# The first projection unit of a two-block transformer kernel stored as two blocks of 256 columns

## What is computed

```python
z = (x @ w_in).astype(F32)          # x: 256 x 1024, w_in: 1024 x 11016
zA, zB, zC, zD, zG = _split(z[..., :N_COLS_BASE], (RWKV_COLS, HGRN_COLS, MLSTM_COLS, LRU_COLS, GATE_COLS))
...
xr, gate = _split(zD, (BRANCH_WIDTH, BRANCH_WIDTH))   # 512 columns each
xc = _causal_conv(xr, conv_w, conv_b)
```

## Time and profile before

| | us |
|---|---|
| median of 3 runs | 1740.6 (1738.82 to 1742.21) |
| the profiled execution, its own time | 1739.38 |
| its span, first to last instruction | 1737.6 |
| PE busy in the span | 1700.8 (98%) |
| VectorE (DVE) busy | 570.5 (33%) |
| ScalarE (ACT) busy | 261.1 (15%) |
| bytes moved by DMA | 540.46 MB, 311 GB/s in the mean |

### The profile page before, as it was taken

How to read it: one execution, slowest core, us unless ns; L and a number is a source line. 1 busy time by engine, 2 the same in 40 slices (tenths; PEclk the granted TensorE clock), 3 DMA queues, 4 the chain that set the end, 5 groups by cost and what they waited for, 6 DMA issues and landing times.

```text
span 1737.6 us, 24288 instructions
## 1 busy us (share of the span) xinstructions
PE 1700.8 (98%) x10121; PEld 997.3 (57%) x10121; DVE 570.5 (33%) x1070; ACT 261.1 (15%) x446; POOL 28.9 (2%) x42
## 2 busy tenths in 40 slices
PE   8999999999999999999999999999999989999998
PEld 7787888888643433333333333433333338998885
DVE  2784377454341111111111111111121235536603
ACT  0323115002011111101010101101010121112200
POOL 1000000100000000000000000000000000000000
PEclk9999999999999999999999999999999999999999
DMA  8564332545799999999999999999999995532331
GB/s 320 191 257 183 146 122 100 166 164 191 270 404 424 421 424 427 427 427 428 428 427 428 426 428 427 428 428 427 426 428 427 428 418 205 194 146 102 141 143 46
DMA packets 65257, 540.46 MB, mean 311 GB/s; under 512 B 5514, under 2 KB 14276, under 8 KB 35744
## 3 DMA queue, kind: packets, MB, share of 16 engines
q1 hardware_dynamic: 58464, 527.31, 74.0%
q10 hardware_dynamic: 4560, 5.90, 1.2%
q0 software_dynamic: 2160, 6.17, 1.1%
HBM read 533.57 MB, written 5.78 MB: 310 GB/s over the span
## 4 chain that ended last, share of the span: by engine, by line
PE 91%; DMA 5%; DVE 2%; ACT 1%; issue 1%; SPq 0%; DVEq 0%; ACTq 0%
PE small L1440 24%; PE small L1482 12%; PE proj L816 10%; PE proj L1590 6%; PE proj L1002 5%; DMA arena<-in_expert_w_gu 4%; PE proj L1666 4%; PE proj L1415 3%; PE small L1388 3%; PE small L1427 2%; PE small L1447 2%; PE small L1081 2%; PE small L837 2%; PE proj L826 2%; PE proj L1529 2%; PE small L1547 2%
## 5 line engine op out<-in xcount | busy, mean ns | idle before, releaser
L1440 PE MATMUL small<-arena 128*64 128x512 f32 x2048 | 447.1, 593 | 6.8 <-DMA arena<-in_expert_w_gu 4.3
L1440 PEld LDWEIGHTS small<-arena 128*64 128x64 f32 x2048 | 151.1, 137 | 287.4 <-issue 274.5
L1482 PE MATMUL small<-arena 128*64 128x512 f32 x1024 | 226.8, 595 | 8.6 <-ACT arena L1924 7.9
L2593 DVE TENSOR_SCALAR arena<-small 128x512 f32<-128x512 f32 x32 | 22.1, 692 | 544.3 <-PE small L1447 544.3
L816 PE MATMUL proj<-arena 128*128 128x256 f32 x832 | 183.2, 380 | 0.9 <-DMA arena<-in_w_in_first 0.9
L816 PEld LDWEIGHTS proj<-arena 128*128 128x128 f32 x832 | 157.0, 190 | 23.1 <-DMA arena<-in_w_in_first 1.3
L1482 PEld LDWEIGHTS small<-arena 128*64 128x64 f32 x1024 | 74.5, 137 | 138.8 <-issue 138.8
L1590 PE MATMUL proj<-arena 128*128 128x128 f32 x896 | 100.5, 275 | 0.5 <-ACT arena L1982 0.5
L1590 PEld LDWEIGHTS proj<-arena 128*128 128x128 f32 x896 | 100.3, 192 | 1.1 <-ACT arena L1982 0.7
L1749 ACT ACTIVATE arena<-proj 128x512 f32<-128x512 f32 (+2 forms) x76 | 43.7, 593 | 361.1 <-PE proj L816 118.4
L1920 ACT ACTIVATE arena<-arena 128x512 f32<-128x512 f32 x32 | 20.1, 629 | 495.0 <-DVE arena L2593 495.0
(11 more groups left out here) (455 smaller groups left out, 1576.6 us busy)
## 6 DMA issues: line engine op xcount, KB each, us to landing
arena<-in_expert_w_gu SPq DMA_DIRECT2D x128, 2048.0 KB, 20.6
arena<-in_expert_w_down SPq DMA_DIRECT2D x31, 2048.0 KB, 28.0
arena<-in_expert_w_down SPq DMA_DIRECT2D x33, 1536.0 KB, 30.3
arena<-in_w_in_first SPq DMA_DIRECT2D x20, 2048.0 KB, 8.5
arena<-in_w_in SPq DMA_DIRECT2D x16, 2048.0 KB, 7.3
arena<-in_expert_w_down SPq DMA_DIRECT2D x33, 512.0 KB, 19.8
arena<-in_w_ada SPq DMA_DIRECT2D x6, 2048.0 KB, 9.9
arena<-in_w_branch SPq DMA_DIRECT2D x4, 2048.0 KB, 8.2
```

The costliest lines, as they stand in the source:

```text
L1440: mm = pe.matmul(bank[CAP * half:CAP * half + CAP, :], XG[:, k % 4, k // 4, :], w[:, k % 4, n * D + half * W:n * D + half * W + W], start= ...
L1482: mm = pe.matmul(y_bank[CAP * half:CAP * half + CAP, :], HM[:, m, u, :], w[:, half * W:half * W + W], start=u == 0 and m == 0, stop=u == 1 ...
```

## The change

The host stores the first unit as two blocks of 256 columns (`[T] * 2` in place of one `W` in the list of widths): for each partition 8 rows k of 256 floats for the first half, then the same for the second. On the chip the slot holds it in the same order, as (2, 8, 256) in place of (8, 512). So each of the five pieces of `D xr` is one run per partition: 1, 2, 2 and 3 KB for the four of the first half, 8 KB for the second half. The issues stay in number, order, queue and bytes; the matmuls stay the same and take their weights from the new places.

```diff
@@ unit_source
-            col = {"D xr": D_COL, "D gate": D_COL + W, "C q": C_COL, "C k": C_COL + W, "C v": C_COL + 2 * W,
+            if name == "D xr":
+                return w_in[:, KD * D_COL:KD * (D_COL + W)].rearrange("p (h k n) -> p h k n", h=2, n=T), (2, KD, T)
+            col = {"D gate": D_COL + W, "C q": C_COL, "C k": C_COL + W, "C v": C_COL + 2 * W,
@@ sync
-                    sp.dma_start(weights(name)[:, :, T:W], src[:, :, T:W]).then_inc(sig("unit_in_0"), 16)
+                    sp.dma_start(weights(name)[:, 1], src[:, 1]).then_inc(sig("unit_in_0"), 16)
@@ tensor, ones_channels
-                            mm = pe.matmul(ps[:, m * T:m * T + T], w[:, k, (2 * b + m) * P:(2 * b + m + 1) * P],
-                                           XT[:, k, :], start=k == 0, stop=k == KD - 1)
+                            lhs = w[:, b, k, m * P:m * P + P] if what == "D xr" else w[:, k, (2 * b + m) * P:(2 * b + m + 1) * P]
+                            mm = pe.matmul(ps[:, m * T:m * T + T], lhs, XT[:, k, :], start=k == 0, stop=k == KD - 1)
@@ tensor, D xr 0
-                        mm = pe.matmul(ps[:, m * T:m * T + T], w[:, k, m * P:m * P + P], XT[:, k, :], start=k == 0 and m == 0, stop=k == KD - 1,
+                        mm = pe.matmul(ps[:, m * T:m * T + T], w[:, 0, k, m * P:m * P + P], XT[:, k, :], start=k == 0 and m == 0, stop=k == KD - 1,
@@ scalar
-                act.dma_start(weights("D xr")[:, ks, 0:T], unit_source("D xr")[0][:, ks, 0:T]).then_inc(sig(f"first_in_{q}"), 16)
+                act.dma_start(weights("D xr")[:, 0, ks, :], unit_source("D xr")[0][:, 0, ks, :]).then_inc(sig(f"first_in_{q}"), 16)
@@ kernel
-            a = by_units(padded_gates(a), [W] * 3 + [256] + [W] * 8 + [32] + [W] * 10)
+            a = by_units(padded_gates(a), [W] * 3 + [256] + [W] * 8 + [32] + [T] * 2 + [W] * 9)
```

## The result

The changed kernel took **1743.54 us** in the median of 20 runs (1739.95 to 1745.43), against 1740.18 (1738.69 to 1742.21) for the kernel before on the same chips: a ratio of 1.0015, 95% interval 1.0009 to 1.0021. It is slower, by 1.6 to 3.7 us or some 0.15%, and lies outside the range of the prediction, which ended at 1742.3.

The account below looks back on a forecast made before the run. PE, busy 98% of the span, was taken as the bound, with 2.42 us of early weight waits recoverable. Savings of 0.8 and 0.3 us made 1.1: 1740.6 - 1.1 = 1739.5 us, range 1737.2 to 1742.3.

Parts of the forecast that it names:

- Gain of 1.1 us at D xr 1: At the front: the second half lands at 14.0, so PE starts D xr 1 then, not at 15.14.
- the savings per run: Second half's landing: 0.8 us from its own longer runs plus 0.3 from the first half's, together 1.1, at most 1.6.
- If the long runs hold those back by a microsecond, it is hidden.: Small vectors on ACT's queue, wanted by PE's transpose at 29: a delay of a microsecond costs nothing.
- rival (c): Front: SP's long runs crowd out the first half's last piece; D xr 1 up to 1.4 us later, 1742.0; chance 0.09.
- D gate's slack, no cost: D gate load: landed at 19.6, needed at about 21.1 after the change, so 1.5 us of slack and no cost.
- Issue of line 618 at 0.4 us: SP's issue of the second half: about 0.4 us in place of 937 ns, with nothing gained.
- my worst case: Front: the whole second half goes first, the first half's last piece lands at 14.0, D xr 1 starts at 16.5.
- VectorE's first copy at 28.3: After PE's transpose: VectorE's first copy moves with PE, to about 28.3 in place of 29.37.
- So 1.1 us arrives whole, with no multiple of it.: From front to kernel end: the 1.1 us gained at the front passes fully to the total, not multiplied.
- the clock as never falling: Whole kernel: PE's granted clock never falls, so a change pays only by shortening one of PE's few waits.
- Chances: Whole kernel: same 0.90, faster and slower 0.05 each; forecast gain of 0.4 to 1.7 us 0.58, something unshown 0.04.

Follow-up runs that it names:

- e2: Changed kernel with only the first half of D xr in long runs, the second half in 1 KB runs: 1738.08 us, and 1738.34 when repeated.
- e11: Changed kernel with the SP queue's load of D gate held back until the small vectors have landed: 1741.26 us.
- e1: Changed kernel with only the second half of D xr in 8 KB runs, the first half's pieces in 1 KB runs: 1750.49 us.
- e3: Changed kernel with the 18 small vectors packed by the host into one array and loaded by one DMA: 1739.18 us.
- e5: Changed kernel, DMAs untouched, with PE doing the first half of D gate 1 ahead of the two transposes: 1739.05 us.
- e10: Changed kernel with its 18 vector loads, the second half of D xr read in four 2 KB runs per partition: 1739.67 us.
- e4: Kernel before, DMAs untouched, with PE held ahead of its first transposes until VectorE has done two memsets: 1745.35 us.
- e7: Kernel before, DMAs untouched, with PE held ahead of its first transposes until VectorE has done one memset: 1741.81 us.

## Why the prediction was wrong, point by point

- *Gain of 1.1 us at D xr 1.* Right in size (15.14 to 14.04), by luck. I had the second half land at 14.0 and bind; it landed at 12.3, and PE bound, with 13 loads at the slow start in place of 10. The landing was mis-sized because I let the savings per run add up (1.1, at most 1.6) and left out who shares the engines: at one packet for one, the queue with the 8 and 16 KB packets got 1.22 MB from 9 to 12 us and ACT's 0.10 (0.81 and 0.27 before). A part of the 2.8 us by which the half came sooner was taken from the ACT queue; the rest came with the longer packets, as both queues together moved 1.32 MB in place of 1.07.
- ***"If the long runs hold those back by a microsecond, it is hidden."*** This is the step that failed. The vectors were held back by 8.2 us (21.5 to 29.7), against a slack of 7.3 less the 1.1 that PE was early, and PE waited 1.95 us. I had named the right queue, the right consumer and no price. The price was in the mechanism that I gave rival (c): turns by run. If each of the 18 loads puts a row and a completion on the first engine, and the uneven counts from 18 to 24 us speak for it, that is some 36 turns, and from 11 us a turn is a 16 KB packet (0.6 us by the earlier trace rows). This count of turns is an estimate that no run shows by engine; that the long packets held the vectors back, e2 (last vector at 21.4) and e11 (by 15.67) show.
- *Rival (c).* The right mechanism with the wrong victim. The piece of the first half came at 11.5, not near 10 as I had it, but before the 12.6 from which it would have cost something. With short runs (e1) it came at 23.9, and D xr 1 13.6 us late and not 1.4. The second half did not go first as a whole, as in my worst case: from 9 to 9.5 us the queues moved 24 and 26 packets on 16 engines, and 23 and 24 from 13 to 14 us, under two an engine in the mean, so they alternated run by run.
- *D gate's slack, no cost*: right (landed 17.3, used at 20.9). *Issue of line 618 at 0.4 us*: wrong, 886 ns against 937, and without effect. *VectorE's first copy at 28.3*: wrong, 30.14, for the wait ahead of it.
- *"So 1.1 us arrives whole, with no multiple of it."* Right for a gain, as e2, e3 and e5 show within their scatter. Wrong for a wait: one of 1.95 us cost 3.6 in the profiled execution, since the clock fell behind it. I had read the clock as never falling, from a row of nines, and not asked what a new gap would do to it. A 9 is 90% or more of a slice of 43 us, which hides a fall of 3.4 us; the kernel before has one at 1429 (0.88 from 1426 to 1440), and the slow loads from 4.5 to 8.9 us are the clock too.
- *Chances.* I gave no case to a new wait behind the front. It would have needed a rival of its own: what does each queue lose when another gets long packets?

## What to carry to other kernels

Making one queue's runs longer did not only make that queue faster here, it left fewer turns to the other: 142 packets from 9 to 12 us in place of 419. Look for the small transfers in flight at the same time, and estimate their delay as their packets per engine, times the longest packet that they will meet (here 16 KB, 0.6 us by the earlier trace rows; the packets per engine no run shows). What worked here was to lengthen the runs of the piece that is needed first (e2, 1738.08 us), to keep what runs beside it in packets of about the same size (e10, 1739.67), or to pack the small transfers into one (e3, 1739.18), against 1743.54 for the changed kernel. And price a new wait of PE at more than its length: here 2 us of wait could cost 3.6.

## What was not expected of the hardware

- The two queues moved one packet for one in stretches with 8 or 16 KB on the one side and 0.5 to 3 KB on the other: 144 to 142, 102 to 101 (after) and 98 to 97 (e1). With 1 KB on SP's side it was 430 to 351 from 9 to 11 us, and with 2 KB (e10, the same stretch) 339 to 189.
- Issuing a load of 128 runs of 8 KB took SP 886 ns, hardly less than one of 1024 runs of 1 KB (937). Over the other profiles the first took 691 to 913 ns and the second 757 to 937, so the number of runs decided little here.
- By the durations of its weight loads (337 ns, as at 0.5, against 190) TensorE starts at its lower clock level in all 14 profiles and goes up only between 7.4 and 10.7 us, while the profile's rows show 1.00.
- The granted clock fell to 0.5 for 3.4 us behind the waits of 1.95 and 2.90 us (after, e4), at a cost of 1.7 us, and not behind those of 1.71 and 2.04 (e7, e11). In seven of the 14 profiles it falls at the start of the expert stage as well, and in four others for 6.8 us in place of 3.4 at its end. By the profiles, that is what splits the runs of several versions into two groups about 2 us apart, as much as the whole effect under study.
